# Block triangular inverse by levels: half of the columns in products, copies and updates

## What is computed

```python
a_mat = jnp.where(strict, jnp.einsum('bnhid,bnhjd->bnhij', kb, kc) * gamma, 0.0)
t_mat = jax.lax.linalg.triangular_solve(eye + a_mat, eye, left_side=True, lower=True)
u = jnp.einsum('bnhij,bnhjd->bnhid', t_mat, vb)
w = jnp.einsum('bnhij,bnhjd->bnhid', t_mat, kb * jnp.exp(decay)[..., None])
# then, chunk after chunk:
v_new = u_ - w_ @ S;  o = qd @ S + qk_ @ v_new;  S = S * l_ + kd.T @ v_new
```

## Time and profile before

| | us |
|---|---|
| median of 3 runs | 1958.97 |
| lowest, highest run | 1958.24, 1960.51 |
| the profiled execution's own time | 1958.46 |
| its span, first to last instruction | 1956.7 |

### The profile page before, as it was taken

How to read it: one execution, slowest core, us unless ns; L and a number is a source line. 1 busy time by engine, 2 the same in 40 slices (tenths; PEclk the granted TensorE clock), 3 DMA queues, 4 the chain that set the end, 5 groups by cost and what they waited for, 6 DMA issues and landing times.

```text
span 1956.7 us, 28028 instructions
## 1 busy us (share of the span) xinstructions
PE 1856.2 (95%) x11001; PEld 1501.7 (77%) x11001; DVE 1058.6 (54%) x1755; ACT 524.8 (27%) x1031; POOL 717.2 (37%) x444
## 2 busy tenths in 40 slices
PE   6999999999988888889999999999999999999999
PEld 5888878777767778456677777788888888888887
DVE  4288889999857666856656436333123312331233
ACT  5366532111111222346613572200100010001000
POOL 4322133433343223026624423534343444344431
PEclk9999999999988878879999999999999999999999
DMA  7310111222220000300121110111111111111112
GB/s 234 85 34 22 33 37 51 60 91 86 89 95 2 2 2 2 130 12 1 45 87 43 44 33 22 44 54 41 56 43 54 39 57 43 54 37 59 43 43 86
DMA packets 111999, 102.41 MB, mean 52 GB/s; under 512 B 5099, under 2 KB 99358, under 8 KB 111646
## 3 DMA queue, kind: packets, MB, share of 16 engines
q1 hardware_dynamic: 109598, 92.68, 15.5%
q10 hardware_dynamic: 2304, 8.39, 1.1%
HBM read 87.42 MB, written 13.63 MB: 52 GB/s over the span
## 4 chain that ended last, share of the span: by engine, by line
PE 80%; DVE 13%; issue 2%; ACT 2%; SPq 1%; POOL 1%; DMA 0%; DVEq 0%; ACTq 0%; POOLq 0%
PE ps L1289 8%; PE ps L1290 8%; PE ps L1291 8%; PE ps L420 6%; PE ps L421 6%; PE ps L422 6%; PE ps L392 5%; PE ps L394 5%; PE ps L393 5%; PE ps L914 3%; DVE top L1692 3%; DVE cacc L1707 2%; DVE score L1696 2%; PE ps L1009 2%; PE ps L1120 2%
## 5 line engine op out<-in xcount | busy, mean ns | idle before, releaser
L709 POOL TENSOR_TENSOR WS<-WR,zero 128x1024 fp32r<-128x1024 f32 (+1 forms) x119 | 229.2, 1926 | 902.8 <-PE ps L394 338.1
L711 POOL TENSOR_TENSOR WS<-WR,WS 128x1024 fp32r<-128x1024 f32 (+1 forms) x119 | 298.7, 2510 | 9.3
L1289 PE MATMUL ps<-HS,WS 128*128 128x512 f32 x704 | 274.4, 390 | 3.2 <-DVE HS L328 3.2
L1291 PE MATMUL ps<-HS,WS 128*128 128x512 f32 x704 | 273.9, 389 | 0.0
L1290 PE MATMUL ps<-HS,WS 128*128 128x512 f32 x704 | 273.9, 389 | 0.0
L439 DVE TENSOR_TENSOR X<-X,ps 128x512 f32<-128x512 f32 x272 | 184.7, 688 | 155.8 <-PE ps L422 148.9
L1985 DVE TENSOR_TENSOR prod<-sil,ps 128x512 f32<-128x512 f32 x44 | 30.3, 688 | 394.7 <-PE ps L1291 394.7
L392 PE MATMUL ps<-HS,WS 128*128 128x512 f32 (+1 forms) x592 | 235.0, 397 | 7.3 <-ACT raw L1396 3.9
L393 PE MATMUL ps<-HS,WS 128*128 128x512 f32 (+1 forms) x592 | 232.0, 392 | 0.0
L394 PE MATMUL ps<-HS,WS 128*128 128x512 f32 (+1 forms) x592 | 231.9, 392 | 0.0
L1696 DVE MATCH_REPLACE8 score<-top,score 128x1024 f32<-128x1024 f32 (+2 forms) x192 | 168.0, 890 | 0.0
(11 more groups left out here) (280 smaller groups left out, 2996.3 us busy)
## 6 DMA issues: line engine op xcount, KB each, us to landing
WR<-in_w_gu SPq DMA_DIRECT2D x44, 512.0 KB, 3.8
WR<-in_w_in SPq DMA_DIRECT2D x36, 512.0 KB, 3.7
WR<-in_w_down SPq DMA_DIRECT2D x22, 512.0 KB, 3.5
X<-in_x SPq DMA_DIRECT2D x8, 1024.0 KB, 8.3
dsa_spill<-cacc ACTq DMA_DIRECT2D x12, 512.0 KB, 2.6
KW<-in_w_xkv SPq DMA_DIRECT2D x8, 512.0 KB, 4.5
WR<-in_w_out SPq DMA_DIRECT2D x8, 512.0 KB, 3.6
out<-X SPq DMA_DIRECT2D x8, 512.0 KB, 2.6
```

Source lines behind the costliest of these rows:

```text
L709: pool.tensor_tensor(hi, w, bc(zero1[:, 0:1], [P, cols]), ALU.add).then_inc(w_hi, 1)
L711: pool.tensor_tensor(lo, w, hi.bitcast(F32), ALU.subtract).then_inc(w_split, 1)
L1289: pe.matmul(ps[:, b0 + half, :], lo, HS[:, 0, k, c], start=(k == 0), stop=False)
L1291: mm = pe.matmul(ps[:, b0 + half, :], hi, HS[:, 0, k, c], start=False, stop=(k == KT - 1))
```

## The change

The products, the copy and the two updates of a level treat 32 columns of each unit instead of 64, packed side by side in the first 256 columns of the PSUM bank. The stationary operand of each matmul keeps its 64 columns. Since the third product uses Y as the stationary operand, Y must have zeros in its other columns: it gets a buffer of its own for each of the levels 1 to 4 (`Ylev`, 128 x 4 x 512, at 32 KB, over `WS` slot 0), which POOL sets to zero once. The split of unit 39, whose slot that is, moves to chunk 13, and the load of unit 42, which waits for it, moves behind three transfers in SP's order.

```diff
+        Ylev = at("Ylev", [P, 4, BANK], 32)
...
+        ylev_zero = sem("ylev_zero")
...
+        def y_of_level(s):
+            return Ylev[:, s - 1, :] if s < 5 else Ym[:, :]
+
+        def half_blocks(ap, s, second):
+
+            w = 1 << s
+            return ap.rearrange("p (n k) -> p n k", k=2 * w)[:, :, w:2 * w] if second else \
+                ap.rearrange("p (n k) -> p n k", k=2 * w)[:, :, 0:w]
+
+        def packed(ap, s):
+            return ap.rearrange("p (n k) -> p n k", k=1 << s)
...
-            for n in range(RING + 2, N_OUT + 2 * RING):
+            for n in range(RING + 2, N_OUT + 2 * RING - 1):
                 load(n)
...
             sp.dma_start(zS[:, :, :], z_dram.rearrange("u p c -> p u c")).then_inc(z_in, 16)
+            load(N_OUT + 2 * RING - 1)
             ta.wait(sp, f"q{TT - 1}")
...
-            for n in range(RING, N_OUT + RING):
+            for n in range(RING, N_OUT + 2):
                 split_of(n)
...
+                    if b == 0:
+                        pool.memset(Ylev[:, :, :], 0.0).then_inc(ylev_zero, 1)
                 elif part == "mask":
...
-            gdn_order(prep, lambda c: None, scan_s, lambda part, e0, e1: None)
+            def dsa(part, e0, e1):
+                if part == "on":
+                    gp.wait(pool, "w1", 3)
+                    split_of(N_OUT + 2)
+
+            gdn_order(prep, lambda c: None, scan_s, dsa)
...
-                    def tri(bank, lhs, rhs):
+                    def tri(bank, lhs, rhs, second):
                         return per_unit(b, lambda ul, par, r: pe.matmul(
-                            ps[r, bank, ul * CHUNK:(ul + 1) * CHUNK], lhs[r, ul * CHUNK:(ul + 1) * CHUNK],
-                            rhs[r, ul * CHUNK:(ul + 1) * CHUNK], start=True, stop=True))
+                            packed(ps[r, bank, ul * 32:(ul + 1) * 32], s), lhs[r, ul * CHUNK:(ul + 1) * CHUNK],
+                            half_blocks(rhs[r, ul * CHUNK:(ul + 1) * CHUNK], s, second), start=True, stop=True))
...
-                        gp.mark(tri(0, gam[:, s % 2, :], TTm[:, B, :]), f"y{s}", b)
+                        gp.mark(tri(0, gam[:, s % 2, :], TTm[:, B, :], True), f"y{s}", b)
...
-                        gp.mark(tri(1, Tm[:, :], Ym[:, :]), f"zt{s}", b)
+                        gp.mark(tri(1, Tm[:, :], y_of_level(s), True), f"zt{s}", b)
                         if s < 5:
-                            gp.mark(tri(2, Ym[:, :], Tm[:, :]), f"z{s}", b)
+                            gp.mark(tri(2, y_of_level(s), Tm[:, :], False), f"z{s}", b)
...
-                    ga.mark(act.activation(Ym[:, :], ps[:, 0, :], ACT.Copy), part, b)
+                    if b == 0 and s == 1:
+                        act.wait_ge(ylev_zero, 1)
+                    ga.mark(act.activation(half_blocks(y_of_level(s), s, True), packed(ps[:, 0, 0:256], s), ACT.Copy), part, b)
...
-                    gd.mark(dve.tensor_tensor(TTm[:, B, :], TTm[:, B, :], ps[:, 1, :], ALU.subtract), f"TT{s}", b)
+                    tt = half_blocks(TTm[:, B, :], s, True)
+                    gd.mark(dve.tensor_tensor(tt, tt, packed(ps[:, 1, 0:256], s), ALU.subtract), f"TT{s}", b)
...
-                        gd.mark(dve.tensor_tensor(Tm[:, :], Tm[:, :], ps[:, 2, :], ALU.subtract), f"T{s}", b)
+                        tm = half_blocks(Tm[:, :], s, False)
+                        gd.mark(dve.tensor_tensor(tm, tm, packed(ps[:, 2, 0:256], s), ALU.subtract), f"T{s}", b)
```

More of the change, by code:

```diff
@@ L1450, in prep @@
                 elif part[0] == "y":
+                    s = int(part[1])
                     gp.wait(act, part, b)
-                    ga.mark(act.activation(Ym[:, :], ps[:, 0, :], ACT.Copy), part, b)
+                    if b == 0 and s == 1:
+                        act.wait_ge(ylev_zero, 1)
+                    ga.mark(act.activation(half_blocks(y_of_level(s), s, True), packed(ps[:, 0, 0:256], s), ACT.Copy), part, b)
                 elif part == "w":
```

## The result

| | before | after |
|---|---|---|
| median of the runs, us | 1958.61 (4 runs) | 1978.82 (4 runs, 1978.15 to 1984.90) |
| profiled execution, its span | 1958.46, 1956.7 | 1978.53, 1976.7 |
| mean granted clock of PE | 0.967 | 0.951 |

The change makes the kernel slower: ratio 1.0108, 95% interval 1.0087 to 1.0129, where 1950.3 (0.996) was forecast. The DVE and ACT work fell as planned, PE's busy time rose. First the page of the changed kernel, then the groups of the updates and of ACT's copy; they answer to the earlier trace rows.

The account below looks back on a forecast made before the run. It took DVE to bound batch 0 after level 1, PE and DVE alternating in batches 1 to 3. Savings of 4.5 (DVE), 4.0 (PE) and 0.2 (ACT), 8.7 us, gave 1949.8, as median 1950.3; range 1944 to 1957.

Parts of the forecast that it names:

- The DVE updates: TT and T updates cut from 512 to 256 columns: 17 on the path, 0.262 us less each, 4.5 us saved.
- The cover: Batch 0 levels: DVE, needing 3.98 us after the edit, still outlasts PE and ACT's 2.9 us, so DVE stays the limit.
- The PE groups: Level products with half the moving columns: 27 groups on the path at 0.12 us, 3 at 0.24, 4.0 us saved.
- rival 1: Level products on PE give nothing because the stationary side sets the pace; 4.7 us remain, 1954.3 us; chance 0.25.
- The sign: Whole kernel: faster by over 3.9 us at 0.80, no change 0.15, slower 0.05.
- rival 4: Batches 1 to 3, y1 to z2: PE waits a larger share and drops to half clock; about 1965 us; chance 0.06.
- The tail: From "w" of batch 3 to the end: a change of more than 1 us would prove the prediction wrong.
- The hidden parts: POOL's 1.85 us fill, the split moved to chunk 13 and the moved load lie under waits and cost 0.

Follow-up runs that it names:

- e1_dve_only: The kernel before with only the DVE updates cut to half of the columns, 256 instead of 512; 1954.97 us, ratio 0.9981.
- e10_burst: The change plus 20 idle-purpose matmuls of 512 streamed columns in a row directly ahead of y1 of batch 0; 1976.04 us, a single execution.
- e5_wide_pe: The change with its products back at 64 columns a unit, copy (but for level 5's) and updates picking their half by stride; 1958.43 us, ratio 0.9987.
- e4_contig: The change with products of levels 1 to 4 reading and writing the first 32 columns of each unit in one run; 1980.97 us, ratio 1.0114.
- e3_pe_only: The change with the DVE updates set back to 512 columns, products and copy still at 32 columns a unit; 1975.23 us, ratio 1.0080.
- e2_house: The change with products, copy and updates back at 64 columns a unit, leaving zeroed Y buffers, fill, moved split and load; 1961.33 us, ratio 1.0010.
- e6_filler: The change plus two idle-purpose matmuls of 512 streamed columns ahead of each of batch 0's 14 groups; 1997.25 us, ratio 1.0188.
- e9_keep: The kernel before with half-width DVE updates and idle-purpose matmuls of 512 streamed columns where PE waits for other engines; 1946.99 us, ratio 0.9928.

## Why the prediction was wrong, step by step

**The DVE updates** were sized right: 0.42 us, as the copy's row said, at all levels. The forecast of 4.5 us stands next to 3.7 in e1_dve_only. That this is on the path at all holds only as long as PE has its clock. The cover was worked out at full clock, 2.9 us of PE and ACT under 3.98 of DVE; at half clock the level's groups and copy take 5.82 us, and in the changed kernel batch 0 is PE's.

**The PE groups** were the mis-sized term: 4.0 us were forecast, 0.12 for a group, and it is 0.02 (0.96 against 0.98 us) at full clock. So the term was worth 27 x 0.02 + 3 x 0.06 = 0.7 us. The interpolation between 1 and 128 moving columns at 128 stationary ones was the wrong step. With 64 stationary columns, 32 moving ones take nearly as long as 64, at which the row of "w" (64 ns with 128 stationary columns, 36 with 64) had hinted and which I weighed too little. Here rival 1 was right, and the rule of the Trainium skill, TensorEngine Tiling, section Performance Considerations, too: one moving column takes as long as 60, and a dimension that is already small should not be cut. The trace agrees for 32 against 64 moving columns, by the 0.96 and 0.98 us; fewer were not run beside 64 stationary ones. By that rule the forecast would have been 1954.3, wrong as well.

**The sign** came from what I had as rival 4, at 0.06: the clock. The step that failed is the argument against it, that batch 0 had kept 1.00 with PE busy for 8.34 of 12 us. Busy time was read as what holds the clock. The changed kernel has 11.03 of 12 us and the half. The rival's own mechanism, PE waiting a larger share, was wrong too: the clock fell where PE waits least. (Half clock makes PE's work longer and so its waits shorter, but in e10_burst PE waited 0.50 us in all between the burst and the fall.) What differs is the width of the level products, and the experiments leave only that as the cause: the width set back cures it (e5_wide_pe); without strides (e4_contig) and with DVE's old durations (e3_pe_only) the clock is lost all the same, and the moved work alone (e2_house) does not lose it. Why narrow products lose the clock stays open: it is not PE's busy time, and e6_filler leaves the form of the matmuls and the density of their columns. That rival 4 had the sign was luck: it came from the wrong mechanism, and batch 0, where the clock fell first, was the argument against it. Its size was low: 1965 for three batches, where 1978.8 was measured. By its own groups the price was 8 x (2.00 - 1.15) = 6.8 us a batch and not 5, and it had neither batch 0 nor the 7 us at the end. In batch 0 the lost clock costs 5.82 - 3.98 = 1.8 us a level against the forecast; what is beside the groups pays too, "w" of batch 3 with 3.12 instead of 2.05 us.

**The tail.** I had said that a change of more than 1 us behind "w" of batch 3 would prove me wrong; there are 7. For the same PE instructions the clock was 0.71 instead of 0.87 and 0.72 instead of 0.79, which is where 5.3 of the 7 us go. The moved split and load are not the cause, as e2_house shows. Nor does a loss of this size belong to every kernel with narrow products: in e3_pe_only and e4_contig, which have them and the split and load too, "w" of batch 3 starts at 796.2 and 802.3 us, and only 1.7 and 1.2 us are lost behind it. What differs is how long this later work has half clock; that this follows from how late and in what state the batches leave PE is argued, not shown.

**The hidden parts** held. The fill took 1.81 us for 1.85 and POOL still waited 4.39 us afterwards; the split in chunk 13 stood between the two Sl, with 5.70 us of wait left. The following rows are POOL's timeline of the changed kernel.

```profile
564.08 1.81 POOL L786 MEMSET Ylev<- 128x2048 f32 x1
570.28 1.27 POOL L790 TENSOR_TENSOR Am<-Am,Xm 128x512 f32<-128x512 f32 x1 [4.39 <-DVE Am L1804]
...
811.11 2.36 POOL L726 TENSOR_TENSOR WS<-WR,WS 128x1024 fp32r<-128x1024 f32 x1
819.17 1.04 POOL L813 TENSOR_TENSOR Sl<-S,lastb 128x512 f32<-128x512 f32 x1 [5.70 <-DVE S L1844]
```

## What to carry to other kernels

Before narrowing small matmuls, look for a row that prices them at the same stationary width: with 64 stationary columns, 32 moving ones took nearly as long as 64 (0.96 against 0.98 us a group), and the narrower groups lost the full clock, which everything beside them paid for. Read the granted clock stretch by stretch next to the busy time; a PE that is 92% busy at 0.50 is a warning sign. Where small, dependent stages run at half clock, wide matmuls into an unused bank, placed where PE waits anyway, gave more (14 us by themselves, and 24 with more of them and the shorter updates) than any of the work taken out. They did not help between narrow groups.

## What the runs showed of the hardware that was not expected

- Granted clock 0.50 with PE busy for 11.03 of 12 us, and 1.00 with 8.34 of 12. The Trainium skill, TensorE: Matmul & The Clock Gate, section Why this matters for your kernels, advises to keep TensorE busy without gaps; the trace disagrees that this is enough: in e6_filler PE was busy for 6.00 of 6 us between 600 and 606 us, at 0.50.
- Two wide matmuls ahead of every narrow group did not restore the clock (e6_filler), while the same matmuls, fewer of them, among 64-column groups kept it at 1.00 (e9_keep).
- A wide filler pair costs 1.15 us between narrow groups at half clock (580.27 less 579.12 us, the starts of the pair and of the group behind it in e6_filler), and 0.66 us at full clock in e9_keep's chain.
